# Gathering the expert inputs feature-major for two packs at once in a two-layer decoder step

## The chip, the cores and the metric

The kernel runs on one core of one Trainium2 chip. The metric is the device time of one execution in microseconds (us), as the median of several runs. The five engines are named as in the profile: PE is the matrix engine's products, PEld its weight loads, DVE the vector engine, ACT the scalar engine, POOL the GpSimd engine, and SP the queue that issues nearly all loads.

## The reference

One step of a decoder trunk of two layers over 288 tokens: 256 prompt tokens and 32 decode tokens (8 sequences of 4). Layer 0 mixes with a gated convolution, layer 1 with retention; both have cross-attention into 256 memory tokens, and both end in the mixture of experts that the change is about:

```python
def hier_moe(h, w_group, w_router, w_gate_up, w_down):
        ...
        g = jnp.argmax(lg, axis=-1)
        ...
        topv, topi = lax.top_k(pe, TOP_K_IN_GROUP)
        wts = topv / jnp.sum(topv, axis=-1, keepdims=True) * pg_sel[:, None]
        ...
        gate = jnp.sum(jax.nn.one_hot(eidx, N_EXPERTS, dtype=jnp.float32) * wts[..., None], axis=1)
        gu = jnp.einsum('td,edf->tef', hs, w_gate_up)
        act = jax.nn.silu(gu[..., :EXPERT_FF]) * gu[..., EXPERT_FF:] * gate[..., None].astype(hs.dtype)
        return jnp.einsum('tef,efd->td', act, w_down)
```

Each token picks one of 4 groups and in it 2 of 8 experts (32 experts, model width 1024, expert width 256). Everything is float32.

## The kernel before

**Layout.** The residual `xT` is held feature-major: 8 tiles (KD) of 128 features by 288 tokens. The mixture of experts does not run every expert on every token. It gives each expert 32 slots (CAP) and works through the 32 experts in 8 packs (PACKS) of 4 experts (PK), so that a pack has 128 slots. A pack whose experts have more than 32 tokens would take a further pass (the `spill` code), which these inputs do not need.

**One pack, in the order of PE's program (`experts`).**
1. `gate_up_chunk`, four times: 8 feature tiles by 4 experts, each product a 128x32 piece of `xgT` (the pack's tokens, feature-major) against 512 columns of weights (line 604).
2. `pick(i + 1)`: the tokens of the next pack are gathered by products with a one-hot matrix. Six products: the one-hot of 128 tokens by 128 slots stands as weights, and 512 features of the token rows `htok` move (line 582). There are three token blocks (128, 128 and 32 tokens) and two halves of the features. The result is slot-major (`xg`), so it has to be turned.
3. In packs 1, 3 and 5 of layer 0: `memory_kv`, keys and values for layer 1 (lines 401 and 406), work that fills the stage.
4. `turn_gates`, `turn_act` (lines 620, 625).
5. `combine(i - 1)`: eight products that spread the previous pack's rows back to the tokens (line 636); DVE adds them to `xT` (line 1397).
6. `turn_x(i + 1)`: eight 128x128 transposes of `xg` (line 630); ACT and DVE copy the banks out twice, once between `pick` and `turn_x` (lines 1102, 1410), once behind it (lines 1106, 1414).
7. `down_half`, twice (line 614).

The last pack differs: `combine(i - 1)` stands ahead of its fourth `gate_up_chunk`, and its own `combine` is split around the second `down_half`.

**Ahead of the packs.** `project_out` (line 496) makes the residual of the eight feature tiles. Between its products it calls `turn_scaled` (line 521), which turns one feature tile to token rows by three transposes, and `partial_sums` (lines 530, 534). `last_sums` (lines 543, 548) closes the router's logits and the tokens' mean squares. `route` makes the ranks of the tokens in their experts by three products (lines 562 to 565); around them stand `memory_kv(1, 0)` and `memory_kv(1, 1)` in layer 0 and three filling products in layer 1. DVE turns the ranks into one-hot matrices (`chosen_slots`).

**Loads.** All weights come through a ring of 7 slots of 2 MB, in the order of `SEQ`: per pack four `gu` chunks and two `dn` chunks, with one `kv1` chunk in packs 1, 3 and 5 of layer 0. SP issues the load of a chunk when the chunk 7 places earlier in the ring has been used (`wait_used`, issue at line 357), strictly in order. Five `gu` chunks (`EXTRA`) have places of their own beside the ring (line 344). In layer 0 the first load behind the ring's first seven, `gu` (0, 1, 0), waits for the slot of `kv1` 0, which is free at the end of `memory_kv(1, 1)`; in layer 1 it waits for the last tile of `project_out`.

## Time and profile before

| | us |
|---|---|
| median of 3 runs | 1237.73 (1232.91 to 1238.44) |
| the profiled execution, its own time | 1237.39 |
| its span, first to last instruction | 1235.6 |
| PE busy | 1170.5 (95%) |
| DVE busy | 356.5 (29%) |
| ACT busy | 154.2 (12%) |
| mean granted clock of TensorE | 0.986 |
| moved by DMA | 364.59 MB, mean 295 GB/s |

PE is busy nearly all the time, but a share over the whole span mixes stages. The two mixtures of experts lie at about 321 to 558 us and 1013 to 1226 us. A float32 product appears in the trace as two records, a transpose as one. In the views below, a "chain" is followed back from the last instruction, each step to what released it.

### The profile page before, as it was taken

Reading aid. Unit: us, or ns where it says so; the run is one execution under the profiler, and the core shown is the slowest. Engines: PE = TensorE matmul, PEld = TensorE weight load, DVE = VectorE, ACT = ScalarE, POOL = GpSimd, SP = SyncE. Lnnn points to the kernel's source line nnn. Section 1 sums busy time; section 2 is a strip of 40 time slices with the busy share of each in tenths; the row PEclk is TensorE's granted clock in tenths of the full one; section 3 lists DMA queues with packets and bytes.
Section 4 is the critical chain, followed back from the end, with each engine's and each line's share of the span. In section 5 each row is a group of like instructions: output and inputs, shape, how many; then the busy total and the mean of one; then the engine's idle time right before and its main releaser. Section 6 shows DMA issues by size and latency. Waiting matters only on the chain.

```text
span 1235.6 us, 13751 instructions
## 1 busy us (share of the span) xinstructions
PE 1170.5 (95%) x5928; PEld 689.7 (56%) x5928; DVE 356.5 (29%) x870; ACT 154.2 (12%) x363; POOL 11.8 (1%) x22
## 2 busy tenths in 40 slices
PE   6999999999999998989999999999999999997886
PEld 5567776677554342436655656566667753432333
DVE  4222224112213141335224242424301022432225
ACT  2000002012111110110201011010200021110002
POOL 0000000000000000000000000000000000000000
PEclk9999999999999999999999999999999999999898
DMA  9953336833599999999234657392985469999994
GB/s 384 427 186 136 136 136 282 340 136 136 234 426 424 428 429 427 429 426 427 109 136 191 243 190 294 137 356 115 414 363 186 155 245 428 412 428 427 427 428 169
DMA packets 28159, 364.59 MB, mean 295 GB/s; under 512 B 3280, under 2 KB 3296, under 8 KB 5056
## 3 DMA queue, kind: packets, MB, share of 16 engines
q1 hardware_dynamic: 25200, 339.87, 67.2%
q10 hardware_dynamic: 1712, 19.17, 3.7%
q0 software_dynamic: 1184, 4.63, 1.0%
q8 instruction: 49, 0.80, 0.3%
q14 instruction: 14, 0.11, 0.0%
HBM read 339.34 MB, written 24.32 MB: 294 GB/s over the span
## 4 chain that ended last, share of the span: by engine, by line
PE 85%; DMA 12%; DVE 2%; issue 1%; ACT 1%; SPq 0%; DVEq 0%
PE bank L766 23%; PE bank L496 13%; DMA ring<-in_gu 11%; PE bank L604 7%; PE bank L582 5%; PE bank L401 5%; PE bank L849 5%; PE bank L406 4%; PE bank L636 4%; PE bank L614 3%; PE bank L820 1%; PE bank L452 1%; PE bank L930 1%; PE bank L419 1%; PE bank L475 1%; PE bank L911 1%
## 5 line engine op out<-in xcount | busy, mean ns | idle before, releaser
L766 PE MATMUL bank<-hT,ring 128*128 128x288 f32 x1088 | 268.2, 407 | 0.9 <-issue 0.9
L766 PEld LDWEIGHTS bank<-hT,ring 128*128 128x128 f32 x1088 | 205.7, 190 | 66.9 <-issue 12.0
L496 PE MATMUL bank<-arena,ring 128*128 128x288 f32 x640 | 158.5, 407 | 1.8 <-DVEq L1305 1.8
L496 PEld LDWEIGHTS bank<-arena,ring 128*128 128x128 f32 x640 | 120.2, 190 | 34.2 <-issue 2.2
L604 PE MATMUL bank<-ring,arena 128*32 128x512 f32 x944 | 115.3, 629 | 24.2 <-DMA ring<-in_gu 24.2
L582 PE MATMUL bank<-arena 128*128 128x512 f32 (+1 forms) x192 | 96.5, 628 | 0.2 <-DVE arena L1380 0.2
L604 PEld LDWEIGHTS bank<-ring,arena 128*32 128x32 f32 x944 | 30.4, 113 | 101.2 <-issue 82.5
L636 PE MATMUL bank<-arena 128*128 128x288 f32 x256 | 68.8, 413 | 2.8 <-issue 2.4
L401 PE MATMUL bank<-arena,ring 128*128 128x256 f32 x256 | 60.1, 398 | 9.4 <-DMA ring<-in_wkv 9.4
L582 PEld LDWEIGHTS bank<-arena 128*128 128x128 f32 (+1 forms) x192 | 31.5, 189 | 65.0 <-issue 63.9
L1397 DVE TENSOR_TENSOR xT<-xT,bank 128x288 f32<-128x288 f32 x128 | 58.2, 455 | 33.0 <-PE bank L636 29.2
L401 PEld LDWEIGHTS bank<-arena,ring 128*128 128x128 f32 x256 | 51.1, 201 | 17.7 <-DMA ring<-in_wkv 9.4
L636 PEld LDWEIGHTS bank<-arena 128*128 128x128 f32 x256 | 46.2, 190 | 24.2 <-issue 8.0
L614 PE MATMUL bank<-ring,arena 128*32 128x512 f32 x512 | 58.7, 596 | 1.0 <-DVE arena L1440 1.0
L849 PE MATMUL bank<-ring,hT 128*128 128x512 f32 x128 | 57.2, 597 | 0.0
L406 PE MATMUL bank<-ring,arena 128*128 128x512 f32 x128 | 55.6, 594 | 0.0
L1525 DVE SCALAR_TENSOR_TENSOR ring<-ring,bank 128x512 f32<-128x512 f32 x64 | 39.7, 682 | 46.2 <-PE bank L820 46.2
L1313 DVE TENSOR_TENSOR xT<-xT,bank 128x288 f32<-128x288 f32 x16 | 7.3, 455 | 154.7 <-PE bank L496 154.7
L406 PEld LDWEIGHTS bank<-ring,arena 128*128 128x128 f32 x128 | 24.2, 190 | 30.8 <-issue 30.7
L849 PEld LDWEIGHTS bank<-ring,hT 128*128 128x128 f32 x128 | 23.8, 190 | 30.8 <-issue 30.4
L1391 DVE SCALAR_TENSOR_TENSOR arena<-arena,bank 128x256 f32<-128x256 f32 x16 | 6.7, 419 | 111.1 <-ACT arena L1115 111.1
L614 PEld LDWEIGHTS bank<-ring,arena 128*32 128x32 f32 x512 | 14.8, 109 | 32.2 <-issue 30.6
(245 smaller groups left out, 846.4 us busy)
## 6 DMA issues: line engine op xcount, KB each, us to landing
ring<-in_gu SPq DMA_DIRECT2D x59, 2048.0 KB, 22.0
ring<-in_dn SPq DMA_DIRECT2D x32, 2048.0 KB, 19.8
ring<-in_rin SPq DMA_DIRECT2D x14, 2048.0 KB, 13.2
ring<-in_cin SPq DMA_DIRECT2D x8, 2048.0 KB, 24.5
ring<-in_kc SPq DMA_DIRECT2D x8, 2048.0 KB, 7.7
ring<-in_vc SPq DMA_DIRECT2D x8, 2048.0 KB, 10.5
ring<-in_st SPq DMA_DIRECT2D x8, 2048.0 KB, 10.4
out_rs<-ring ACTq DMA_DIRECT2D x8, 2048.0 KB, 8.4
```

The lines of the kernel that those rows point to most:

```text
L401: mm = pe.matmul(bank[KV_BANKS[i][j]][:, o * NM:(o + 1) * NM], w[:, k, f:f + P], src[:, k, :], start=(k == 0), stop=(k == KD - 1), skip_gr ...
L406: mm = pe.matmul(bank[KV_BANKS[i][j]][:, :], src[:, k, mb * P:(mb + 1) * P], w[:, k, :], start=(k == 0), stop=(k == KD - 1))
L419: mm = pe.matmul(bank[0][32 * h:32 * h + 32, 0:NM], qm[:, 2 * h + dt, 32 * b:32 * b + 32], k2[:, bi, 2 * h + dt, :], start=(b == 0 and dt ...
L496: mm = pe.matmul(bank[1 + o % 4][:, 0:T], w[:, k, :], cat[:, k, :], start=(k == 0), stop=(k == kt - 1))
L582: mm = pe.matmul(bank[n][:, :], sel[0:m, b, :], htok[b][0:m, n * 512:(n + 1) * 512], start=(b == 0), stop=(b == 2))
L604: mm = pe.matmul(bank[2][32 * e:32 * e + 32, :], xt[:, k, 32 * e:32 * e + 32], wv[e // 2][:, e % 2, kk, :], start=(k == 0), stop=(k == KD ...
L614: mm = pe.matmul(bank[5 + n][32 * e:32 * e + 32, :], actT[:, f, 32 * e:32 * e + 32], wv[:, e, f, :], start=(f == 0), stop=(f == 1), skip_g ...
L636: return pe.matmul(bank[b][:, 0:T], yo[:, o * P:(o + 1) * P], GT, start=True, stop=True)
L766: mm = pe.matmul(outs[o], w[:, o, k, :], src[:, k, :], start=(k == 0), stop=(k == KD - 1))
L849: mm = pe.matmul(bank[4 + b][:, :], hT[:, k, b * P:(b + 1) * P], w[:, k, :], start=(k == 0), stop=(k == KD - 1))
L1397: return dve.tensor_tensor(xT[:, o, :], xT[:, o, :], bank[b][:, 0:T], ALU.add)
L1525: dve.scalar_tensor_tensor(out=st[:, j, dt, :], in0=st[:, j, dt, :], scalar=float(np.exp(NS * LOGG[h])), in1=bank[j][:, :], op0=ALU.mult, ...
```

## The change

- `turn_scaled` makes two transposes and one plain product: the 32 decode tokens of feature tile k go to partitions 32 (k // 2) to 32 (k // 2) + 31, so that the decode rows `htok3` fill four partition quarters with 256 features each. `token_sums` writes the decode tokens' sums of squares to all four quarters (six products for three).
- The ranks take five products for three; two of them make the decode ranks and the decode choice for every quarter, with a new constant `tri3` of 128 columns (`iota` and `valid` go). DVE copies the decode choice out and makes the decode ranks in an instruction of its own.
- `picked`, `turn_picked`, `pick` and `turn_x` go, and so does `xg`. Instead the token rows stand as weights and the one-hot of two packs (256 columns) moves: `gather_prompt`, four calls of four products, and `gather_decode`, eight products with 32 rows each, one per partition quarter and column half. The result is feature-major already; ACT and DVE copy each bank out once, two feature tiles by two packs.
- The gather for packs 2j and 2j+1 stands in pack 2j-1; that for packs 0 and 1 is spread over the head and pack 0. In even packs `combine(i - 1)` is split in five and three tiles, around the transposes.
- `combine` takes banks by pack (`SPREAD`); `yo`, `xgT` and the one-hots move to other places in the arena. The order of the loads, the ring and the places beside it stay as they are.

```diff
-    cols = [("ident", P), ("ones", P), ("tri", P), ("iota", NE), ("cos", T), ("sin", T),
-            ("decay", H * 2 * P), ("dmask", TD), ("inner", H * NS), ("tail", 2 * H), ("kvm", 2 * H), ("fold", P),
-            ("neghalf", 3), ("valid", 3), ("thr", PASSES - 1), ("slots", CAP)]
+    cols = [("ident", P), ("ones", P), ("tri", P), ("cos", T), ("sin", T),
+            ("decay", H * 2 * P), ("dmask", TD), ("inner", H * NS), ("tail", 2 * H), ("kvm", 2 * H), ("fold", P), ("tri3", P),
+            ("neghalf", 3), ("thr", PASSES - 1), ("slots", CAP)]
...
-        SPREAD = ((2, 3, 4), (0, 1, 4))
+        X_BANKS = (0, 1, 5, 6)
+        SPREAD = {i: (2, 3, 4) if i % 2 == 0 else (0, 1, 4, 6) for i in range(PACKS)} | {PACKS - 2: (0, 1, 4),
+                                                                                         PACKS - 1: (2, 3, 4)}
...
                 if k >= 2:
                     pe.wait_ge(S("htok_out"), KD * i + k - 1)
-                for b, (t0, n) in enumerate(BLK):
-                    mm = pe.transpose(bank[5 + 2 * (k % 2)][0:n, b * P:(b + 1) * P], hT[:, k, t0:t0 + n], C("ident"))
-                mm.then_inc(S("h_turned"), 1)
+                for b in range(2):
+                    pe.transpose(bank[5 + 2 * (k % 2)][:, b * P:(b + 1) * P], hT[:, k, b * P:(b + 1) * P], C("ident"))
+                g = slice(32 * (k // 2), 32 * (k // 2) + 32)
+                pe.matmul(bank[5 + 2 * (k % 2)][g, 2 * P:3 * P], hT[:, k, TP:T], C("ident"), start=True, stop=True,
+                          skip_group_check=True).then_inc(S("h_turned"), 1)
+
...
+            def token_sums(k):
+
+                for b in range(2):
+                    pe.matmul(bank[1][:, b:b + 1], sq[:, k, b * P:(b + 1) * P], C("ones")[:, 0:1],
+                              start=(k == 0 and b == 0), stop=(k == KD - 1), skip_group_check=True)
+                for g in range(4):
+                    mm = pe.matmul(bank[1][32 * g:32 * g + 32, 2:3], sq[:, k, TP:T], C("ones")[:, 0:1],
+                                   start=False, stop=(k == KD - 1), skip_group_check=True)
+                return mm
...
-                pe.matmul(bank[5][:, 0:3 * NE], C("tri"), M, start=True, stop=False, skip_group_check=True)
-                pe.matmul(v3(bank[5][:, NE:3 * NE], 2), C("ones"), M[:, 0:1, :].to_broadcast([P, 2, NE]), start=False,
+                ranks = v3(bank[5][:, 0:4 * NE], 4)
+                pe.matmul(ranks[:, 0:2, :], C("tri"), M[:, 0:2, :], start=True, stop=False, skip_group_check=True)
+                pe.matmul(ranks[:, 1:3, :], C("ones"), M[:, 0:1, :].to_broadcast([P, 2, NE]), start=False,
                           stop=False, skip_group_check=True)
-                pe.matmul(bank[5][:, 2 * NE:3 * NE], C("ones"), M[:, 1, :], start=False, stop=True,
+                pe.matmul(ranks[:, 2, :], C("ones"), M[:, 1, :], start=False, stop=False, skip_group_check=True)
+                pe.matmul(ranks[:, 2, :], C("tri3", TD), M[0:TD, 2, :], start=False, stop=True, skip_group_check=True)
+                pe.matmul(ranks[:, 3, :], C("fold", TD), M[0:TD, 2, :], start=False, stop=True,
                           skip_group_check=True).then_inc(S("ranks"), 1)
...
-            def picked(sel, n):
-
-                for b, (t0, m) in enumerate(BLK):
-                    mm = pe.matmul(bank[n][:, :], sel[0:m, b, :], htok[b][0:m, n * 512:(n + 1) * 512],
-                                   start=(b == 0), stop=(b == 2))
+            def gather_decode():
+
+                for q in range(2):
+                    for g in range(4):
+                        r = slice(32 * g, 32 * g + 32)
+                        pe.matmul(bank[X_BANKS[g]][:, 256 * q:256 * q + 256], htok3[r, P * q:P * q + P],
+                                  onehot_m[r, 2, :], start=(q == 0), stop=False, skip_group_check=True)
+
+            def gather_prompt(m):
+
+                for b in range(2):
+                    for q in range(2):
+                        k = 2 * m + q
+                        mm = pe.matmul(bank[X_BANKS[m]][:, 256 * q:256 * q + 256], htok[b][:, k * P:(k + 1) * P],
+                                       onehot_m[:, b, :], start=False, stop=(b == 1), skip_group_check=True)
                 return mm
...
-            def turn_picked(n, src):
-                for k in range(4):
-                    mm = pe.transpose(bank[n][:, k * P:(k + 1) * P], src[:, (4 * n + k) * P:(4 * n + k + 1) * P],
-                                      C("ident"))
-                return mm
-
...
-                def pick(i):
-                    pe.wait_ge(S("selected"), PACKS * L + i + 1)
-                    for n in range(2):
-                        picked(onehot_m, n).then_inc(S("x_picked"), 1)
-
-                def turn_x(i):
-                    pe.wait_ge(S("xg_out_a"), PACKS * L + i + 1)
-                    turn_picked(0, xg).then_inc(S("xg_turned"), 1)
-                    pe.wait_ge(S("xg_out_d"), PACKS * L + i + 1)
-                    turn_picked(1, xg).then_inc(S("xg_turned"), 1)
+                def gather(j):
+
+                    pe.wait_ge(S("selected"), PACKS * L + 2 * j + 2)
+                    pe.wait_ge(S("y_out_a"), PACKS * L + 2 * j - 1)
+                    pe.wait_ge(S("y_out_d"), PACKS * L + 2 * j - 1)
+                    gather_decode()
+                    for m in range(4):
+                        gather_prompt(m).then_inc(S("x_done"), 1)
+
+                def gathered(c):
+                    pe.wait_ge(S("xt_out_a"), 9 * L + min(c + 1, 3))
+                    if c == 3:
+                        pe.wait_ge(S("xt_out_d"), 7 * L + 1)
 
                 def combine(i, part=range(KD)):
 
+                    banks = SPREAD[i]
+                    n = len(banks)
                     pe.wait_ge(S("gt_out"), PACKS * L + i + 1)
                     for o in part:
                         if o == 0:
                             pe.wait_ge(S("y_out_a"), PACKS * L + i + 1)
                         if o == 0 and i:
                             pe.wait_ge(S("y_added"), KD * PACKS * L + KD * i)
-                        if o == 4:
+                        if o == (4 if i == PACKS - 1 else 0):
                             pe.wait_ge(S("y_out_d"), PACKS * L + i + 1)
-                        if o == 1 and i != PACKS - 2:
+                        if o == 1 and 3 in banks:
                             pe.wait_ge(S("actT_out"), PACKS * L + min(i + 2, PACKS))
-                        if o >= 3:
-                            pe.wait_ge(S("y_added"), KD * PACKS * L + KD * i + o - 2)
-                        spread(o, SPREAD[i == PACKS - 2][o % 3]).then_inc(S("spread"), 1)
-
-                pe.wait_ge(S("htok_scaled"), 3 * (L + 1))
-                pick(0)
-                turn_x(0)
+                        if o >= n:
+                            pe.wait_ge(S("y_added"), KD * PACKS * L + KD * i + o - n + 1)
+                        spread(o, banks[o % n]).then_inc(S("spread"), 1)
+
-                pe.wait_ge(S("htok_scaled"), 3 * (L + 1))
-                pick(0)
-                turn_x(0)
+                pe.wait_ge(S("selected"), PACKS * L + 1)
+                pe.wait_ge(S("htok_scaled"), 3 * L + 1)
+                gather_decode()
+                pe.wait_ge(S("selected"), PACKS * L + 2)
+                pe.wait_ge(S("htok_scaled"), 3 * L + 3)
+                for m in range(2):
+                    gather_prompt(m).then_inc(S("x_done"), 1)
                 for i in range(PACKS):
                     if i == PACKS - 1:
                         pe.wait_ge(S(f"npass{L}"), 1)
                         more = pe.value_load(npass[0:1, L:L + 1], min_val=0, max_val=PASSES - 1)
-                    pe.wait_ge(S("xt_out_a"), PACKS * L + i + 1)
+                    if i and i % 2 == 0:
+                        pe.wait_ge(S("xt_out_a"), 9 * L + i + 3)
+                        pe.wait_ge(S("xt_out_d"), 7 * L + i + 1)
                     if i >= 2:
                         pe.wait_ge(S("y_added"), KD * PACKS * L + KD * (i - 1))
                     for c in range(4):
-                        if c == 2:
-                            pe.wait_ge(S("xt_out_d"), PACKS * L + i + 1)
+                        if i == 0:
+                            gathered(c)
                         if c == 3 and i == PACKS - 1:
                             combine(i - 1)
-                        gate_up_chunk(c, gate_up_landed(L, i, c), xgT).then_inc(S("gu_sum"), 1)
+                        gate_up_chunk(c, gate_up_landed(L, i, c), xgT[:, :, P * (i % 2):P * (i % 2) + P]) \
+                            .then_inc(S("gu_sum"), 1)
+                        if i == 0 and c < 2:
+                            gather_prompt(2 + c).then_inc(S("x_done"), 1)
                     if i == 0:
                         count_chosen()
-                    if i + 1 < PACKS:
-                        pick(i + 1)
+                    if i == 1:
+                        pe.wait_ge(S(f"npass{L}"), 1)
+                    if i % 2 and i + 1 < PACKS:
+                        gather((i + 1) // 2)
+                    if i and i % 2 == 0:
+                        combine(i - 1, range(5))
                     if L == 0 and i == 0:
                         pe.wait_ge(S("kv1_out"), 2)
                     if L == 0 and i in MEMORY_IN:
@@ -698,11 +742,15 @@
                     turn_gates().then_inc(S("gt_turned"), 1)
                     pe.wait_ge(S("act_ready"), PACKS * L + i + 1)
                     turn_act().then_inc(S("act_turned"), 1)
-                    if i and i < PACKS - 1:
+                    if i % 2 and i < PACKS - 1:
                         combine(i - 1)
-                    if i + 1 < PACKS:
-                        turn_x(i + 1)
+                    if i and i % 2 == 0:
+                        combine(i - 1, range(5, KD))
                     pe.wait_ge(S("actT_out"), PACKS * L + i + 1)
+                    if i and i % 2 == 0:
+                        pe.wait_ge(S("y_added"), KD * PACKS * L + KD * i)
+                    if i % 2 and i + 1 < PACKS:
+                        pe.wait_ge(S("xt_out_a"), 9 * L + i + 4)
...
-                for b, (t0, n) in enumerate(BLK):
-                    act.activation(htok[b][0:n, :], htok[b][0:n, :], ACT.Copy, scale=rstd3[0:n, b:b + 1]) \
-                       .then_inc(S("htok_scaled"), 1)
+                for b, rows in ((2, htok3), (0, htok[0]), (1, htok[1])):
+                    act.activation(rows, rows, ACT.Copy, scale=rstd3[:, b:b + 1]).then_inc(S("htok_scaled"), 1)
...
+                def gathered_out(j, m):
+                    act.wait_ge(S("x_done"), 16 * L + 4 * j + m + 1)
+                    act.activation(xgT[:, 2 * m:2 * m + 2, :], v3(bank[X_BANKS[m]][:, :], 2), ACT.Copy) \
+                       .then_inc(S("xt_out_a"), 1)
+
+                for m in range(3):
+                    gathered_out(0, m)
...
-                def select(i):
-                    chosen_slots(PK * i).then_inc(S("selected"), 1)
+                def select(j):
+                    chosen_slots(2 * PK * j, 2 * PK, slice(2, 3)).then_inc(S("selected"), 1)
+                    chosen_slots(2 * PK * j, 2 * PK, slice(0, 2)).then_inc(S("selected"), 1)
```

## Rows read from the trace of the kernel before

**Rows 1.** The page, part 2: DMA share in tenths and GB/s, in 40 slices of 30.9 us.
```profile
DMA  9953336833599999999234657392985469999994
GB/s 384 427 186 136 136 136 282 340 136 136 234 426 424 428 429 427 429 426 427 109 136 191 243 190 294 137 356 115 414 363 186 155 245 428 412 428 427 427 428 169
```
**Rows 2.** The page, part 4: the chain that ended last, by line.
```profile
PE bank L766 23%; PE bank L496 13%; DMA ring<-in_gu 11%; PE bank L604 7%; PE bank L582 5%; PE bank L401 5%; PE bank L849 5%; PE bank L406 4%; PE bank L636 4%; PE bank L614 3%; PE bank L820 1%; PE bank L452 1%; PE bank L930 1%; PE bank L419 1%; PE bank L475 1%; PE bank L911 1%
```
**Rows 3.** Windows of 10 us: length, then PE, PEld, DVE, ACT, POOL busy (instructions), granted clock, DMA share, GB/s.
```profile
310.00:320.00 10.00, 10.00 (x51) 8.89 (x50) 3.07 (x15) 2.84 (x13) 0.00 (x0) 1.00 0.00 0
...
330.00:340.00 10.00, 10.00 (x66) 3.62 (x59) 1.44 (x6) 0.98 (x2) 0.00 (x0) 1.00 1.03 434
...
530.00:540.00 10.00, 7.79 (x69) 2.62 (x62) 1.00 (x2) 0.35 (x1) 0.00 (x0) 1.00 1.00 425
...
1060.00:1070.00 10.00, 10.00 (x84) 3.02 (x76) 1.54 (x3) 0.96 (x2) 0.00 (x0) 1.00 0.95 374
```
**Rows 4.** Timeline of the SP queue: start us, length, issues of loads, with count.
```profile
302.02 0.33 SPq L357 DMA_DIRECT2D ring<-in_dn  x1
321.11 0.33 SPq L357 DMA_DIRECT2D ring<-in_gu  x1
...
1004.68 0.33 SPq L357 DMA_DIRECT2D ring<-in_gu  x1
...
1041.08 19.23 SPq L357 DMA_DIRECT2D ring<-in_dn  x2
```
**Rows 5.** The chain in order of time, 296 to 345 us: start us, length, line, records.
```profile
296.68 0.48 PE bank L521 x3
...
299.10 0.49 PE bank L530 x6
...
313.89 0.20 PE bank L565 x2
314.09 6.99 PE bank L401 x32
...
342.99 0.87 PE bank L630 x8
```
**Rows 6.** The same chain, packs 2 and 3 of layer 0.
```profile
391.41 5.93 PE bank L582 x12
398.77 3.66 PE bank L636 x14
403.30 3.57 PE bank L614 x32
406.87 6.87 PE bank L604 x64
413.74 5.93 PE bank L582 x12
419.67 13.95 PE bank L406 x32
```
**Rows 7.** The same chain in layer 1: products with 32 rows, four partition quarters at once.
```profile
652.43 1.07 PE bank L820 x8
```
**Rows 8.** Timeline of PE: start us, length, line, records, [idle before <- releaser].
```profile
537.05 1.92 PE L604 MATMUL bank<-ring,arena 128*32 128x512 f32 x16 [2.21 <-DMA ring<-in_gu]
538.91 4.15 PE L636 MATMUL bank<-arena 128*128 128x288 f32 x16
...
1172.59 1.92 PE L604 MATMUL bank<-ring,arena 128*32 128x512 f32 x16 [2.34 <-DMA ring<-in_gu]
1177.39 2.89 PE L604 MATMUL bank<-ring,arena 128*32 128x512 f32 x16 [2.88 <-DMA ring<-in_gu]
...
1201.95 3.55 PE L604 MATMUL bank<-ring,arena 128*32 128x512 f32 x16 [2.08 <-DMA ring<-in_gu]
```
**Rows 9.** Windows of 2 us, columns as in rows 3.
```profile
1202.00:1204.00 2.00, 2.00 (x12) 0.65 (x16) 0.00 (x0) 0.00 (x0) 0.00 (x0) 0.53 0.96 410
...
1206.00:1208.00 2.00, 2.00 (x10) 1.53 (x9) 1.67 (x4) 0.00 (x0) 0.00 (x0) 1.00 0.98 418
```

172 lines of the change are left out of this document (80 added, 92 removed).

## Prediction

> **What bounds the kernel now.** I read the page first. PE is busy 95% of the span and the product lines fill the chain by line, so on the page this looks like a PE kernel from which 6% of gathering (5% in line 582, more in line 630) could be cut. But that line also holds 11% of "DMA ring<-in_gu" [rows 2], and the slices show where it lies: DMA stands at 9 in slices 11 to 18 and 33 to 38, with 412 to 430 GB/s, which is exactly where the two mixtures of experts run [rows 1]. Everywhere else the share is mostly 3 to 6. So I took windows of 10 us. Layer 0: DMA idle at 310 to 320, share 1.00 or more in every window from 330 to 560 (the first and one of the last stand in the rows). PE is also full at 330, but not at 530, where it is busy 7.79 of 10 us. Layer 1 is the same from 1010 to 1210, with one dip to 0.95 and 374 GB/s at 1060 [rows 3]. A share of 1.00 at 427 GB/s is the most that this transfer path shows anywhere in the run.
>
> The timeline of PE says who waits for whom: PE stands before a gate-up product until the `gu` chunk has landed, 2.21 us at 537.05, and in layer 1 2.34, 2.88 and 2.08 us (six more waits of over 1 us, at 470.79, 475.58, 1113.89, 1118.69, 1143.24 and 1148.04, are not shown) [rows 8]. So at the end of both stages the stream of weights is late, not PE.
>
> A balance shows the same. A chunk of 2.10 MB at 427 GB/s takes 4.9 us. A pack is six chunks, 29.5 us; two packs of layer 0 with a `kv1` chunk are 13 chunks, 63.9 us. On PE, a pack repeats after 413.74 - 391.41 = 22.3 us, and one with `memory_kv` takes some 14 us more [rows 6]: 58.7 us for two packs of layer 0 and 44.7 for two of layer 1. PE is the faster of the two already. It looks full in layer 0 because it starts behind: the stage begins with seven loaded slots to eat.
>
> Hence the rule that I use: the end of each stage is the time at which SP may issue the first load of the stream, plus a fixed number of bytes at 427 GB/s, plus what PE does behind the last landings. The first issues are at 321.11 (released by the end of `memory_kv(1, 1)`, which starts at 314.09 and takes 6.99 us [rows 5]) and at 1004.68 (released by the last tile of `project_out`) [rows 4].
>
> **The gather itself: a large saving under cover.** Removed for two packs: 2 x 5.93 us of line 582 [rows 6] and 2 x 0.87 us of line 630 [rows 5], 13.6 us. Added: 16 products with 256 columns, 32 records. The trace has such a record in line 401, 6.99 / 32 = 0.218 us [rows 5], so 7.0 us. The 8 decode products have 32 rows each in four quarters; line 820 has such products with 512 columns, 8 records in 1.07 us [rows 7]. Here 16 records of half the columns, again 1.07 us. If the quarters did not run together it would be 16 x 0.218 = 3.5 us. Sum 8.1 us (bound 10.5): two packs become 5.5 us shorter, 22 us per layer, 44 us in all. One copy out for each bank in place of two shortens ACT and DVE, which wait anyway. All of this lies behind the stream of weights and I cost it at nothing: PE will only wait longer for `gu` chunks. The cover is 63.9 - 53.2 us for two packs in layer 0 and 58.9 - 39.2 us in layer 1; nothing short of those would bring the gather back on the path.
>
> One place gains. In layer 1 the second `dn` load of pack 2 is issued 19 us after the first, at about 1060 [rows 4], when the first half of pack 1's `down_half` frees the slot, and the queue had run dry: the dip at 1060. With the head and pack 0 having one gather of 8.1 us in place of two picks and two turns, and pack 1 8.1 in place of 6.8, PE gets there some 4.5 us sooner, and the dip goes. It is worth 0.5 us by the share (5% of 10) and 1.3 us by the rate (12% of 10) [rows 3]; I take 0.9.
>
> **The order in odd packs.** The eight-microsecond gather now stands ahead of `down_half`, in layer 0 with 14 us of `memory_kv` behind it. Does a slot come free too late? A `dn` chunk lands 9.8 us behind the last `gu` chunk; PE then has 8.1 + 14 + 1 + 3.7 us to do before `down_half` ends 3.6 us later, 18 us behind the landing. The ring allows six chunks, 29.4 us. So nothing runs dry. The wait for the copies of banks 5 and 6 ahead of `down_half` has `turn_act` and `combine` over it, some 5 us against a copy of 0.7. Free.
>
> **What is added ahead of the stream.** This is on the path, since PE is full there and the first load waits for it.
> - `turn_scaled`: three records take 0.48 us [rows 5]. The third, a transpose in one record, becomes a product in two: one more record of 128 columns, 0.11 us from 0.87 / 8 for the transposes of line 630. I take 0.12, bounds 0.08 and 0.2. Seven calls lie before the issue in layer 1 (0.84 us), eight in layer 0 (0.96 us).
> - `token_sums`: six records take 0.49 us [rows 5]; now twelve, of which eight are narrow and in four column quarters. I take +0.3 us a call, bounds 0.1 and 0.8. One call in layer 1, two in layer 0.
> - Ranks: two more products, each 0.20 us like line 565 [rows 5]: +0.4 us (0.2 to 0.6), in layer 0 only, since in layer 1 the first load has been issued by then.
> - The constants grow by 93 columns, 48 KB at 384 GB/s [rows 1]: +0.12 us at the start.
> Together layer 0 +1.96 us (1.0 to 3.8), layer 1 +1.14 us (0.7 to 2.2), start +0.12. DVE's extra copy and its own instruction for the decode ranks stand before the first gather, not before a load: hidden.
>
> The Trainium skill (TensorEngine Tiling, Tiling Modes, Key Properties) says that changing the tiling mode drains the engine, which speaks against four-quarter products between full ones. The trace has the case: 1.07 us for the 8 records of line 820 where their columns alone need 0.85. A drain of 0.2 us at each change would add some 2 us more before each stream; the upper bounds above hold about half of that.
>
> **Behind the last landing.** The code there is the same: gate-up chunk 2 at 537.05 and 1201.95, then `combine(6)`, chunk 3, the turns and the down halves. What may change is PE's clock. At 1201.95 the same 16 records take 3.55 us, against 1.92 at 537.05 [rows 8]; the granted clock is 0.53 there, that is mostly 1.2 GHz, and 1.00 again under `combine(6)`, 2.4 GHz [rows 9]. PE had waited 2.08 us before it, and 2.21 us before the fast one, so equal waits end either way. The change makes PE wait about 3 us before each of pack 7's chunks (4.9 less 1.9), not before one only. In layer 0, where the chunk was fast, I expect the slow one more often than not: +1.3 us, bounds 0 and 3.3 (1.63 for the chunk and as much again for half of `combine`). In layer 1, where it was slow already: 0, bounds -1.6 and +1.7.
>
> **Sum** against the profiled execution's own 1237.39 us: +0.12 +1.96 +1.14 -0.9 +1.3 = +3.6, so 1241.0. The median of the runs is 0.34 above that execution: 1241.3. With all low ends it is 1.1 us less than before, with all high ends 10.6 more.
>
> **The rivals.**
> - *The saving arrives* (faster). If PE set the end of both stages, 44 us would go: about 1194 us. For it: PE is full from 330 to 470 and line 582 is in the chain. Against it: the DMA share in the same windows, and the waits for `gu` behind them. It decides if the stream has slack, and it has only the dip. Chance 0.06.
> - *The clock stays down* (slower). PE in pack 7 works 1.9 of every 4.9 us; if the clock falls in the first wait and doesn't come back until `combine(6)` is over, chunk 2 costs 1.63 us more in layer 0 and `combine(6)` 4.15 us more in both layers: 9.9 in place of 1.3, 1249.9 us. For it: 2.88 us of waiting at 1177.39 already gave 2.89 us for a chunk of 1.92 [rows 8]. Against it: each slow chunk in the trace is followed by work at or near full speed. It decides where PE's busy share in pack 7 falls too low for the grant to return. Chance 0.12.
> The Trainium skill (TensorE: Matmul & The Clock Gate, HAM oscillation) tells of a kernel whose short bursts between transfer waits all ran cold. By that rule every burst of pack 7 would be at 1.2 GHz, as in this rival.
> - *The gather isn't cheaper*: the quarters run one after another, or changes between full and quarter products cost as much as the transposes did. Then two packs take 44.7 or 58.7 us as now, still below the stream: 1241 us as well, and only the lengths in the trace would differ. Chance 0.04.
> - The forecast, stream plus head and tail, has 0.78, with a range of its own from 1236.6 to 1248.4.
>
> **How the numbers follow.** A measurement of this kernel tells about 0.5%, 6.2 us, from no change: below 1231.5 is faster, above 1243.9 slower. Slower: the clock rival's 0.12 and about 0.10 from the forecast's upper half. Faster: 0.07. The range 1235.0 to 1248.0 leaves out the fast rival, most of the clock rival and some of the scatter that the three runs show on the low side.
>
> **What would show each step.** Right: gate-up waits for `gu` of about 3 us each in packs 3 to 7 of both layers; the total of that wait over 60 us; PE's busy time down by some 45 us; DMA at 1.00 from the first issue on without the dip; first issues about 2 us and, in layer 1, a further 1 us later against the stage's start. Wrong: a DMA share below 1.00 inside the stages, a first issue later by more than 4 us, or stages that end earlier against their first issue by more than 2 us.

## The result and the profile after

The changed kernel takes 1249.78 us (median of 4 runs, 1249.41 to 1251.08) against 1236.97 us for the kernel before, run beside it on the same chip: ratio 1.0108, 95% interval 1.0094 to 1.0122. The forecast was 1241.3 us, 1235.0 to 1248.0. It is slower by 12.8 us where I expected 3.6, and outside the range. The profiled execution has a span of 1248.3 us against 1235.6, so the traces show 12.7 of the 12.8 us.

The page of the kernel after: busy time, the GB/s line that answers to [rows 1], the chain by line that answers to [rows 2], and three groups of products of gate-up, the gather and down (busy, mean ns | idle before, releaser).

```profile
PE 1148.7 (92%) x6040; PEld 701.6 (56%) x6040; DVE 341.0 (27%) x854; ACT 146.5 (12%) x347; POOL 11.8 (1%) x22
...
GB/s 383 428 177 135 135 135 319 307 123 135 234 428 427 428 426 427 428 427 399 90 122 196 245 155 333 135 344 114 405 370 162 175 208 428 428 427 427 427 428 163
...
PE bank L812 23%; DMA ring<-in_gu 13%; PE bank L498 13%; PE bank L636 5%; PE bank L403 5%; PE bank L895 4%; PE bank L408 4%; PE bank L604 4%; DMA ring<-in_dn 3%; PE bank L662 3%; PE bank L646 3%; PE bank L866 1%; PE bank L454 1%; PE bank L421 1%; PE bank L976 1%; PE bank L477 1%
...
L636 PE MATMUL bank<-ring,arena 128*32 128x512 f32 x944 | 126.8, 673 | 48.3 <-DMA ring<-in_gu 48.3
...
L604 PE MATMUL bank<-arena 128*128 128x256 f32 x256 | 58.6, 384 | 0.0
...
L646 PE MATMUL bank<-ring,arena 128*32 128x512 f32 x512 | 60.7, 610 | 7.3 <-issue 3.6
```

The share and the rate in both stages are as before (426 to 428 GB/s in most slices), the products of the gather (line 582 before, 604 now) shrink in the chain, and the waits for weights grow in it: gate-up waits 48.3 us for `gu` chunks, and `dn` chunks now bound too. PE is busy 21.8 us less in all. The windows of 10 us answer to [rows 3]: the idle window at 310, the full ones behind it, and at 1060 no dip any more.

```profile
310.00:320.00 10.00, 10.00 (x52) 8.88 (x51) 1.68 (x7) 2.25 (x7) 0.00 (x0) 1.00 0.09 38
...
330.00:340.00 10.00, 10.00 (x76) 4.32 (x68) 0.69 (x1) 0.60 (x1) 0.00 (x0) 1.00 0.99 419
530.00:540.00 10.00, 5.63 (x36) 1.09 (x32) 0.69 (x1) 0.00 (x0) 0.00 (x0) 0.83 1.02 431
...
1060.00:1070.00 10.00, 9.97 (x61) 6.16 (x63) 5.22 (x11) 1.61 (x3) 0.00 (x0) 1.00 1.00 426
```

The gather itself, in the timeline of PE (start us, length, line, records, [idle before <- releaser]). It ends at 424.51, where `memory_kv` begins: 8.1 us from 416.42, as forecast. The three waits above it answer to [rows 6], where PE had none.

```profile
404.80 2.88 PE L636 MATMUL bank<-ring,arena 128*32 128x512 f32 x16 [2.59 <-DMA ring<-in_gu]
409.67 3.27 PE L636 MATMUL bank<-ring,arena 128*32 128x512 f32 x16 [1.99 <-DMA ring<-in_gu]
414.57 1.92 PE L636 MATMUL bank<-ring,arena 128*32 128x512 f32 x16 [1.62 <-DMA ring<-in_gu]
416.42 1.15 PE L596 MATMUL bank<-arena 32*128 32x256 f32 x16
417.50 7.17 PE L604 MATMUL bank<-arena 128*128 128x256 f32 x32
424.51 13.90 PE L408 MATMUL bank<-ring,arena 128*128 128x512 f32 x32
```

**Where 12.7 us came from.** I laid the same marks over both traces: the first issue of each stage [rows 4], the last gate-up chunks [rows 8], and the first product behind the stage.

| stretch | us |
|---|---|
| ahead of layer 0's `project_out` | -0.6 |
| head of layer 0, to the first issue (321.11, now 324.45) | +3.9 |
| stream of layer 0 (537.05, now 540.44, both at full clock) | 0 |
| handover from layer 0 to layer 1 | +6.1 |
| a second wait of PE in layer 1, line 421, at 884 | +0.8 |
| head of layer 1, to the first issue (1004.68, now 1017.91) | +3.0 |
| stream of layer 1, the dip gone | -1.8 |
| tail of layer 1 | +1.2 |

The two first issues, from the timeline of the SP queue:

```profile
324.45 0.33 SPq L359 DMA_DIRECT2D ring<-in_gu  x1
...
1017.91 0.33 SPq L359 DMA_DIRECT2D ring<-in_gu  x1
```

And the handover, from the timelines of PE: the last `combine` of layer 0, then the first product of retention (line 766 before, 812 now). First the kernel before:

```profile
554.86 2.18 PE L636 MATMUL bank<-arena 128*128 128x288 f32 x8 [0.86 <-issue]
558.21 4.12 PE L766 MATMUL bank<-arena,ring 128*128 128x288 f32 x16 [1.17 <-DVE arena L1585]
```

Then the kernel after:

```profile
558.24 2.18 PE L662 MATMUL bank<-arena 128*128 128x288 f32 x8 [0.86 <-issue]
565.86 5.90 PE L812 MATMUL bank<-arena,ring 128*128 128x288 f32 x16 [5.44 <-issue]
```

PE is idle 5.44 us in place of 1.17, no event in the trace releases it ("issue"), and the 16 records behind it take 5.90 us in place of 4.12. This stretch alone is half of the loss, and the prediction has no term for it.

The second wait is small and lies far from any changed product, between line 419 (now 421) and the line behind it. The kernel before, then the kernel after:

```profile
867.05 7.11 PE L419 MATMUL bank<-ring,arena 128*32 128x256 f32 x128 [1.03 <-DVE arena L1256]
874.09 1.99 PE L431 MATMUL bank<-arena 128*128 128x256 f32 x8
...
876.48 7.11 PE L421 MATMUL bank<-ring,arena 128*32 128x256 f32 x127 [1.03 <-DVE arena L1295]
884.01 0.40 PE L421 MATMUL bank<-ring,arena 128*32 128x256 f32 x1 [0.43 <-issue]
884.34 1.99 PE L433 MATMUL bank<-arena 128*128 128x256 f32 x8
```

From start to start that is 7.86 us in place of 7.04. The last record again waits for nothing that the trace shows.

### The profile page after: what moved, and what is told of

It reads as the page before. It is cut to its first block, busy times and chain, and to the rows that moved or that the text cites. A ratio compares the mean times of both kernels' runs of the same rounds, so it can differ in the third digit from the quotient of the medians.

```text
span 1248.3 us, 13951 instructions
## 1 busy us (share of the span) xinstructions
PE 1148.7 (92%) x6040; PEld 701.6 (56%) x6040; DVE 341.0 (27%) x854; ACT 146.5 (12%) x347; POOL 11.8 (1%) x22
## 4 chain that ended last, share of the span: by engine, by line
PE 80%; DMA 16%; DVE 2%; issue 1%; ACT 1%; SPq 0%; DVEq 0%
PE bank L812 23%; DMA ring<-in_gu 13%; PE bank L498 13%; PE bank L636 5%; PE bank L403 5%; PE bank L895 4%; PE bank L408 4%; PE bank L604 4%; DMA ring<-in_dn 3%; PE bank L662 3%; PE bank L646 3%; PE bank L866 1%; PE bank L454 1%; PE bank L421 1%; PE bank L976 1%; PE bank L477 1%
## 5 line engine op out<-in xcount | busy, mean ns | idle before, releaser
L636 PE MATMUL bank<-ring,arena 128*32 128x512 f32 x944 | 126.8, 673 | 48.3 <-DMA ring<-in_gu 48.3
L646 PE MATMUL bank<-ring,arena 128*32 128x512 f32 x512 | 60.7, 610 | 7.3 <-issue 3.6
L662 PEld LDWEIGHTS bank<-arena 128*128 128x128 f32 x256 | 46.2, 190 | 26.2 <-issue 13.0
L604 PE MATMUL bank<-arena 128*128 128x256 f32 x256 | 58.6, 384 | 0.0
L604 PEld LDWEIGHTS bank<-arena 128*128 128x128 f32 x256 | 47.8, 190 | 12.3 <-issue 6.3
```

Source lines behind the costliest of these rows:

```text
L604: mm = pe.matmul(bank[X_BANKS[m]][:, 256 * q:256 * q + 256], htok[b][:, k * P:(k + 1) * P], onehot_m[:, b, :], start=False, stop=(b == 1), ...
L636: mm = pe.matmul(bank[2][32 * e:32 * e + 32, :], xt[:, k, 32 * e:32 * e + 32], wv[e // 2][:, e % 2, kk, :], start=(k == 0), stop=(k == KD ...
L646: mm = pe.matmul(bank[5 + n][32 * e:32 * e + 32, :], actT[:, f, 32 * e:32 * e + 32], wv[:, e, f, :], start=(f == 0), stop=(f == 1), skip_g ...
L662: return pe.matmul(bank[b][:, 0:T], yo[:, o * P:(o + 1) * P], GT, start=True, stop=True)
```

## The experiments

Theory A for the heads: the narrow product of `turn_scaled` costs several times what I gave it. Theory B for the handover: what PE waits for is its own instructions behind the branch that skips the further pass. The rivals were that the head is longer for the sums and the ranks, and that the gather's own work, its waits or the clock made the difference. Ratios are to the kernel before on the same chip.

### The heads: the decode tokens turned by a product or by a transpose

In the kernel after, the plain product goes and a transpose that ends on the same partitions takes its place. Everything else stays.

```diff
-                pe.matmul(bank[5 + 2 * (k % 2)][g, 2 * P:3 * P], hT[:, k, TP:T], C("ident"), start=True, stop=True,
-                          skip_group_check=True).then_inc(S("h_turned"), 1)
+                n = 32 * (k // 2) + 32
+                pe.transpose(bank[5 + 2 * (k % 2)][0:n, 2 * P:3 * P], hT[:, k, T - n:T], C("ident")) \
+                  .then_inc(S("h_turned"), 1)
```

> The changed kernel with its decode turn made by a transpose of the last 32, 64, 96 or 128 tokens of the feature tile, so that the 32 decode tokens still land in their partition quarter but no product on a 32-column part of the array is needed. Theory A (the head): each of the 16 decode turns by a narrow product costs 0.42 us of PE on the path to the first load of a stage (a period of 9.27 us for 8.85), so the first load of layer 0 comes about 3 us earlier than in the changed kernel (324.45 to about 321.4) and of layer 1 another 3 us; the time falls by 6 us to about 1244. Rival: the head is longer for the sums and the ranks; then the first loads move by less than 1 us each and the time stays within 2 us of 1249.8.

Measured: 1241.55 us, ratio 1.0042 (1.0023 to 1.0060), 8.2 us less. The first issues are at 321.92 and 1012.58. The counterpart gives the kernel before the plain product for its third transpose:

```diff
-                for b, (t0, n) in enumerate(BLK):
-                    mm = pe.transpose(bank[5 + 2 * (k % 2)][0:n, b * P:(b + 1) * P], hT[:, k, t0:t0 + n], C("ident"))
-                mm.then_inc(S("h_turned"), 1)
+                for b in range(2):
+                    pe.transpose(bank[5 + 2 * (k % 2)][:, b * P:(b + 1) * P], hT[:, k, b * P:(b + 1) * P], C("ident"))
+                pe.matmul(bank[5 + 2 * (k % 2)][0:TD, 2 * P:3 * P], hT[:, k, TP:T], C("ident"), start=True, stop=True,
+                          skip_group_check=True).then_inc(S("h_turned"), 1)
```

> The kernel before with one thing taken from the change: the turn of the 32 decode tokens of each feature tile is a plain product instead of a transpose; everything else stays. Theory A: the period of a feature tile in project_out grows from 8.85 to about 9.27 us, both stages' first loads come 3 us later each, and the time rises by 5 to 7 us to about 1243. Rival (one more record of 128 columns, 0.11 us): the period grows by 0.12 us and the time by 1.5 to 2 us.

Measured: 1243.03 us, 1.0053 (1.0033 to 1.0074), 6.5 us more, first issues at 323.74 and 1010.57. Sixteen times 0.42 us are 6.7 us, and that is what the kernel before loses. The kernel after gains 1.5 us more; in its trace with the transpose the second wait, at line 421, is gone as well, which is 0.8 us of it. The timeline shows how the 0.42 us come about. After:

```profile
289.28 0.44 PE L523 MATMUL bank<-cst,hT 128*128 128x128 f32 x2
289.65 0.41 PE L525 MATMUL bank<-cst,hT 128*32 128x128 f32 x2
289.99 8.03 PE L498 MATMUL bank<-arena,ring 128*128 128x288 f32 x32
297.94 0.68 PE L515 MATMUL bank<-hT,arena 128*36 128x288 f32 x2
```

With the transpose:

```profile
287.85 0.44 PE L523 MATMUL bank<-cst,hT 128*128 128x128 f32 x2
288.13 0.27 PE L525 MATMUL bank<-cst,hT 128*96 128x128 f32 x1
288.24 7.93 PE L498 MATMUL bank<-arena,ring 128*128 128x288 f32 x32
296.09 0.68 PE L515 MATMUL bank<-hT,arena 128*36 128x288 f32 x2
```

From start to start, the transpose takes 0.11 us, the narrow product 0.34, the two transposes ahead of it 0.37 in place of 0.28, and the 32 records of line 498 take 7.95 in place of 7.85. So the narrow product costs 0.42 us more, and the surplus lies on both of its sides as well as in it. The number of columns alone does not bring it: the transposes for the first two feature tiles have 32 columns too (128*32), and the first of them, in layer 0, also takes 0.11 us (243.90 to 244.01). A plain product of 128 columns in the same place was not tried.

### The handover: the branch, then where its target lies

First the branch of PE alone is taken away, with the further pass that it skips (these inputs never use it).

```diff
-                with pe.If(more > 0):
+                if False:
```

> The changed kernel without the branch in PE's program around the further pass, which is not taken with these inputs; the code of that pass on PE is left out. Theory B (handover): the 5.4 us in which PE stands idle at 560.4 to 565.9, behind the last pack of layer 0 and with the rin chunk landed at 560.0, is a fetch of instructions behind the branch, that has to queue in the full DMA rings. Without the branch that wait is gone or below 1.5 us, the following 16 products run at the full clock (4.1 for 5.9 us), and the time falls by 5 to 6.5 us to about 1244. Rival: PE waits there for data or for another engine; then the idle time stays at 4 us or more and the time within 1.5 us of 1249.8.

> The kernel before without the branch in PE's program around the further pass; that pass's code on PE is left out. Theory B: PE waits only 1.17 us there, for DVE's first scaled tile, so nothing is to be gained: the same within 1 us. If the branch costs something by itself in both kernels, the time falls here too by 2 us or more, and the difference between the two kernels isn't explained by it.

Measured: the kernel after 1243.79 us, 1.0060 (1.0043 to 1.0077), idle 1.18 us and released by DVE, 4.12 us for the product; the kernel before 1236.58 us, 1.0003. So the wait comes with the branch, and only the kernel after pays it. In the kernel after without the branch:

```profile
561.38 4.12 PE L812 MATMUL bank<-arena,ring 128*128 128x288 f32 x16 [1.18 <-DVE arena L1625]
```

Both kernels have the branch. What differs is the code around it. A first pair was to move the code with 128 empty instructions at the start of PE's program (`pe.nop()`).

> The changed kernel with 128 empty instructions at the start of PE's program, where PE waits for its first weights until 9.4 us anyway. Theory B (a fetch of instructions whose cost depends on where the branch's target lies in the fetched blocks): the idle time of 5.4 us at the handover from layer 0 to layer 1 changes, to below 2 us in the likelier case, and the time falls by 4 to 6 us. Rival (a wait for data or an engine): nothing moves, within 1.5 us of 1249.8, since no other work is changed.

> The kernel before with the same 128 empty instructions at the start of PE's program. Theory B: where the target now lies unluckily, an idle time of 4 us or more appears behind the last pack of layer 0 and the time rises by 4 to 6 us; otherwise the same within 1 us. Rival: the same within 1 us in any case.

Measured: 1251.30 and 1235.95 us, idle times as without them. The profile lists as many instructions as for the unshifted kernels (13951 in the one after), and its instruction queue holds as many packets (51 and 49). So nothing shows that the empty instructions moved anything, and the pair tells nothing. A second pair changed how far the branch jumps: in the kernel after the skipped code loses 18 products (six calls of `gather_single`, three products each), in the kernel before it gains fifteen.

```diff
-                            for k in range(KD):
+                            for k in range(2):
                                 mm = gather_single(k)
```

> The changed kernel with the code of the further pass on PE (jumped over, never run with these inputs) shortened by 18 of its 24 gather products, to 67 products, which is fewer than the 75 of the kernel before; the changed kernel has 85. Theory B2: what matters is how far the branch jumps; a near target is fetched already, a far one has to be fetched through the full DMA rings. Then the idle time of 5.4 us behind layer 0 falls to 1.2 us and the time by 5 to 6.5 us, as without the branch. Rival B3 (the branch as such, or its place in the program): the wait stays above 4 us and the time within 1.5 us of 1249.8.

```diff
-                            picked(onehot_m, 0)
+                            for _ in range(6):
+                                picked(onehot_m, 0)
```

> The kernel before with the jumped-over code of the further pass on PE lengthened by 15 products, from 75 to 90, none of which is run. Theory B2: an idle time of 4 us or more appears on PE behind the last pack of layer 0, and the time rises by 5 to 6 us to about 1242. Rival B3: the same within 1 us.

Measured: 1250.88 us with 5.34 us idle, and 1236.54 us with 1.17. The length of the jump alone is not it.

```profile
q8 instruction: 1, 0.02, 6.3%
```

The kernel after, first 535 to 563 us (no q8 line), then 563 to 564, where `combine` had ended at 560.4:

```profile
q1 hardware_dynamic: 824, 11.98, 100.6%
q14 instruction: 1, 0.01, 0.1%
...
q1 hardware_dynamic: 28, 0.43, 99.9%
q8 instruction: 1, 0.02, 6.6%
```

The branch itself stands in the traces at 556.12 us before and at 559.51 after. So before, a fetch comes 5.6 us ahead of the branch; after, none comes in the 24.8 us ahead of it, the next 3.6 us behind it, and PE works 2 us later. A real shift was made with products of one column at PE's start, where it waits until 9.4 us for its first weights:

```diff
+            pe.wait_ge(S("par_in"), 16)
+            for _ in range(24):
+                pe.matmul(bank[7][0:32, 0:1], par[:, 0:32], par[:, 0:1], start=True, stop=True)
             memory_kv(0, 0)
```

> The kernel after with 24 one-column products more at the start of PE's program, where PE waits for the first weights until 9.4 us anyway; they cost nothing there and move everything behind them by 96 instructions. Theory F (what PE waits for at the handover is the fetch of its own instructions behind the branch: the branch of pack 7 comes near the end of a fetched piece of 16 KB, 256 instructions, and its target lies in a piece that is asked for only when PE jumps): the branch now lies behind a piece border, the piece with the target is asked for before the jump, the fetch record at 564.9 us moves to before 558, the idle time ahead of the first product of retention goes from 5.4 us to about 1.2 us, released by DVE, that product takes 4.1 us in place of 5.9, and the time is 1243.5 to 1246 us. Theory G (the wait belongs to the branch itself, or to work that only the kernel after has, wherever the code lies): 5.4 us again, and 1249.5 to 1251.5 us.

> The kernel after with 64 one-column products more at the same free place: 256 instructions, exactly one piece, so that all code lies in its piece where it lay before. Theory F: the wait stays, 5.4 us, and the time is 1249.5 to 1251.5 us. If any insertion at the start removes the wait (theory H, some other effect of the inserted products), the idle time is about 1.2 us here as well, 1243.5 to 1246 us.

> The kernel before with 46 one-column products more at the same free place, 184 instructions. In the kernel before the piece with the branch's target is asked for at 552.2 us, five us ahead of the branch. Theory F: the border moves to behind the branch, the fetch comes only after the jump, and an idle time of 4 to 5.5 us appears ahead of the first product of retention where 1.17 us stood; 1240.5 to 1243 us. Theory G: 1.17 us again, and 1235.5 to 1238 us.

Measured: 24 products in the kernel after, 1243.13 us, 1.0060 (1.0042 to 1.0078); 64 products, a whole piece, 1250.70 us, 1.0133 (1.0107 to 1.0159); 46 products in the kernel before, 1236.74 us, 1.0011. The first two are as theory F says: 96 instructions at a place where PE has nothing to do make the kernel 6.6 us faster than the kernel after (7.6 us faster than its neighbour with 256 on the same chip), 256 do nothing. With 96 the wait at line 421 is gone too, and from the first product of retention to the first issue of layer 1 the kernel takes 3.0 us more than the kernel before, not 3.8; with 256 that wait is there again, 0.43 us. So the second wait hangs on the place of the code as well. The third run missed: no wait came. Counting the products then put some 296 instructions between branch and target in the kernel before and 351 in the kernel after, and gave a sharper rule, which the next two runs were made to break.

> The kernel before with 30 one-column products at the free place at the start, 120 instructions. A count of PE's instructions puts some 296 between the branch and its target in the kernel before and some 351 in the kernel after. The fetch times of the shifted kernels fit one rule (F2): PE holds the piece in which it works and has the next one asked for when it enters it; a jump is free if its target lies in one of these two, and else it waits for a fetch. In the kernel after the branch's piece ends about 58 instructions behind the branch, so the two reach to 314, short of 351; in the kernel before it ends about 146 behind, so they reach to 402, beyond 296; 184 instructions of shift left 218 and 474, still beyond, which is why that run missed. 120 instructions leave 26 and 282, short of 296. F2: an idle time of 4 to 5.5 us ahead of the first product of retention, with a fetch after the jump, and 1240.5 to 1243.5 us. If the kernel before can't be made to wait by a shift (F only an accident of the kernel after): 1.17 us and 1235.5 to 1238 us.

> The kernel after with 58 one-column products, 232 instructions: less than a piece. F2: the branch's piece ends 82 behind the branch, the two reach to 338, short of 351 by a little: the wait stays, 5.4 us, 1249.5 to 1251.5 us. If what counts is only that the branch isn't in the last part of its piece (58 is near the end, 82 less so), it may be gone: 1.2 us, 1243.5 to 1246 us. The count has some twenty instructions of uncertainty, so this one is the nearer call of the two.

Measured: the kernel before with 30 products 1244.50 us, 1.0059 (1.0038 to 1.0080), the kernel after with 58 products 1248.37 us, 1.0078 (1.0059 to 1.0097) with 5.45 us idle. Both waited, as the rule says; the times lie 1.0 us above and 1.1 us below what was expected. The first product of retention, in the timeline of PE. The kernel after with 24 products (with 64 the idle time is 5.30 us):

```profile
561.83 4.12 PE L812 MATMUL bank<-arena,ring 128*128 128x288 f32 x16 [1.18 <-DVE arena L1628]
```

The kernel before with 30 products (with 46 it is 1.17 us):

```profile
564.55 1.78 PE L766 MATMUL bank<-arena,ring 128*128 128x288 f32 x3 [5.72 <-issue]
```

In its DMA view, the window of 561 to 562 us has the fetch, and 535 to 561 has none; `combine` had ended at 558.8 (556.65 + 2.18):

```profile
q8 instruction: 1, 0.02, 6.7%
```

### Is the gather under cover?

In layer 1 the kernel after keeps 4 of 24 products of each gather in packs 1, 3 and 5; the kernel before leaves out two thirds of the one-hot products for packs 1 to 7. Both leave part of the gather undone.

```diff
-                    gather_decode()
+                    if L == 0:
+                        gather_decode()
                     for m in range(4):
-                        gather_prompt(m).then_inc(S("x_done"), 1)
+                        if L == 0:
+                            mm = gather_prompt(m)
+                        else:
+                            mm = pe.matmul(bank[X_BANKS[m]][:, 256:512], htok[1][:, 0:P], onehot_m[:, 1, :], start=True,
+                                           stop=True, skip_group_check=True)
+                        mm.then_inc(S("x_done"), 1)
...
-                for b, (t0, m) in enumerate(BLK):
+                for b, (t0, m) in enumerate(BLK[0:blocks]):
...
-                        picked(onehot_m, n).then_inc(S("x_picked"), 1)
+                        picked(onehot_m, n, 1 if L and i else 3).then_inc(S("x_picked"), 1)
```

> The changed kernel with most of the gather left out in layer 1: of the 24 products of each gather for packs 2 to 7 only four remain. This takes about 6.9 us of PE three times, 20 us in all. The law of the stream (first load plus bytes plus what follows the last landing): the time stays within 1.5 us of 1249.8, and PE only waits 20 us longer for gate-up weights. If PE's work were on the path, the time would fall by up to 20 us.

> The kernel before with two thirds of the one-hot products left out in layer 1, for packs 1 to 7: 4 us of PE a pack, 28 us in all. The law of the stream: at most the dry spot of the load queue at 1060 us goes, so 0 to 2 us faster than before (1235 to 1237), although 28 us of PE work are gone. If PE's work were on the path: up to 28 us faster.

Measured: 1248.49 and 1234.70 us, 1.3 and 1.8 us less than the kernels that they come from. Some 19 us (three gathers, 8.1 us each, less 1.75 us for the four products that stay) and 28 us (two thirds of seven times 5.93) of PE's work bought next to nothing: in layer 1 the saving of the change is hidden as the forecast said, and the stream sets the stage. In layer 0 nothing was left out; there only the traces speak, with a stream of the same length in both kernels.

### Moving the stream forward

If a stage is its first issue plus bytes, bytes moved ahead of it should count in full. Three `gu` chunks beside the ring were put earlier in the order.

```diff
+for moved, ahead_of in ((("gu", (0, 1, 1)), ("gu", (0, 1, 0))), (("gu", (0, 1, 2)), ("gu", (0, 1, 0))),
+                        (("gu", (1, 1, 1)), ("gu", (1, 0, 0)))):
+    SEQ.remove(moved)
+    SEQ.insert(SEQ.index(ahead_of), moved)
```

> The kernel before with three loads moved in SP's order: the two gu chunks of layer 0 that have a place beside the ring go ahead of the chunk that waits for the slot of kv1 0, and one such chunk of layer 1 goes ahead of layer 1's first gu. The law of the stream: 9.8 us of bytes in layer 0 and 4.9 us in layer 1 move into time in which the queue was idle or half used. But PE of the kernel before has only about 6 us of waits in layer 0 to give up, so I expect 5 to 6 us there and 4 to 5 us in layer 1: 1226 to 1229. If the stream doesn't set the end, within 2 us of before.

> The changed kernel with the same three loads moved. Here PE has some 19 us of waits in layer 0 and more in layer 1, so the stream's whole 9.8 + 4.9 us should be gained: 1249.8 - 14.7 = 1235, 13 to 15.5 us faster than the changed kernel. This is where the cheaper gather would first be worth something: its gain from this edit should be 4 us larger than that of the kernel before.

Measured: 1233.27 us, 0.9975 (0.9962 to 0.9988), and 1246.22 us, 1.0086 (1.0057 to 1.0114): 3.5 and 3.6 us less, where 8 to 15.5 were expected; and the kernel after gains no more than the kernel before, where 4 us more were expected of it. Windows of 5 us show the queue running dry elsewhere. The kernel before with the new order, columns as in [rows 3]:

```profile
325.00:330.00 5.00, 4.80 (x47) 1.70 (x49) 1.55 (x3) 0.60 (x1) 0.00 (x0) 1.00 0.34 102
370.00:375.00 5.00, 4.28 (x20) 2.93 (x19) 0.88 (x2) 0.60 (x1) 0.00 (x0) 1.00 0.43 102
1055.00:1060.00 5.00, 5.00 (x52) 1.47 (x48) 1.97 (x4) 0.60 (x1) 0.00 (x0) 1.00 0.55 164
```

Its SP queue explains the second window:

```profile
372.13 0.33 SPq L361 DMA_DIRECT2D ring<-in_dn  x1
```

and its PE timeline the queue, by `memory_kv` of pack 1:

```profile
358.02 14.08 PE L405 MATMUL bank<-arena,ring 128*128 128x256 f32 x64
```

The `dn` load at 372.13 is issued as `memory_kv` ends (358.02 + 14.08 = 372.10). In the first packs the ring waits for PE, so bytes moved forward are partly lost again; that this is the whole difference between 8 or more and 3.5 us was not separated.

### Together

The transpose, the new order and 28 one-column products (24, and 4 for the 16 instructions that the transposes save) in the kernel after:

> The kernel after with all that the runs so far point to: the decode tokens turned by a transpose (8 us), the three loads beside the ring ahead of their packs (3.6 us), and 28 one-column products at the start (24 as in the first run of this group, 4 for the 16 instructions that the transposes save). Theory F: 1250.2 - 8.2 - 3.6 - 5.5 = about 1233 us, 1231 to 1236, level with the kernel before or a little faster. Theory G: the handover keeps its 5.4 us, and 1237 to 1240 us.

Measured: 1232.38 us, 0.9974 (0.9959 to 0.9988). It beats the kernel before, by 3 us, and is level with the kernel before in the new order (0.9975). The feature-major gather, freed of its side costs, is worth nothing measurable here.

## Why the prediction was wrong

**What bounds the kernel: right.** The stages run at the transfer rate from the first issue on (427 GB/s is what they sustain, not the most that shows: [rows 3] has a window at 434), layer 0's stream has the same length within 0.1 us, and taking gather work away in layer 1 changes under 2 us.

**The gather: right.** 8.1 us for two packs against 8.1 forecast, 13.6 before. The quarters do run together (1.08 us from 416.42 to 417.50). The wait for `gu` doubled, from 24.2 to 48.3 us, but did not pass 60: some of the saving went into slower products, some into waits for `dn`. PE's busy time fell by 21.8 and not by 45 us: gate-up was busy for 126.8 us with the same 944 records (115.3 before), down for 60.7 (58.7), and the longer heads and the slow first product of retention add some 9 us, an estimate from the stretches above.

**The dip: right in kind.** It is gone; layer 1's stream is 1.8 us shorter against its first issue, where I took 0.9 of a range to 1.3.

**The heads: right in kind, wrong in size.** The term `turn_scaled` is the step that failed: 0.12 us a call (bounds 0.08 and 0.2) against 0.42, which is +3.4 us in place of 0.96 for eight calls, and 2.9 in place of 0.84 for seven. I had priced a narrow product as one more record of a transpose, the nearest row by columns but not by tile. `token_sums`, at +0.3 us, was too dear: from start to start it is 0.60 against 0.58. The ranks cost 1.23 against 0.58 us, +0.65 for my 0.4. Head of layer 0: +3.9 for 1.96 forecast, just beyond the upper bound of 3.8; layer 1: +3.0 for 1.14, beyond its 2.2. The prediction had quoted the Trainium skill (TensorEngine Tiling, Tiling Modes, Key Properties), that a change of tiling mode drains the engine, and had set a drain aside at some 2 us per stage, half in the bounds. A drain would fit the 0.42 us, which lie on both sides of the product, but the runs do not show one: the transpose of the same 32 columns cost nothing extra, and a weight load that shows was not ruled out.

**The handover: no step at all.** This is the larger of the two failed steps. The sum ended each stage and began the next as if nothing lay between, a term put at nothing without a reason. It cost 6.1 us: 4.3 of waiting and 1.8 of a product at a lower clock behind it (granted clock 0.63 from 565 to 571 us). The second wait adds 0.8. Nothing in the profile of before points to it; its only trace there is a q8 packet at 550 us. What I could have done is to ask of each branch whether the change moves code around it.

**The clock: neither the term nor the rival came.** The chunk ahead of layer 0's last `combine` ran at full clock, so the +1.3 did not come; PE's waits in that pack were 0.49, 2.89 and 1.43 us before the first three chunks, not 3 us before each, and the four chunks took 1.92, 3.50, 1.92 and 1.92 us, so not every burst ran at 1.2 GHz. In the tail of layer 1 the clock moved elsewhere. Two lines of the timeline of PE answer to [rows 8]: the chunk before `combine(6)`, slow before, is fast now, and a `down_half` that waited for its `dn` chunk takes 3.59 us in place of 1.92.

```profile
1213.41 1.92 PE L636 MATMUL bank<-ring,arena 128*32 128x512 f32 x16 [1.69 <-DMA ring<-in_gu]
...
1224.83 3.59 PE L646 MATMUL bank<-ring,arena 128*32 128x512 f32 x16 [1.21 <-DMA ring<-in_dn]
```

The window of 5 us around the second has a granted clock of 0.68:

```profile
1225.00:1230.00 5.00, 4.24 (x20) 1.17 (x16) 0.06 (x1) 1.50 (x2) 0.00 (x0) 0.68 0.22 93
```

The two cancel (-1.6 and +1.7 us); the net of +1.2 us is what PE now waits for the last `gu` and `dn` chunks. `combine(6)` took 4.15 us in both layers, so the rival in which the clock stays down is refuted, though its 1249.9 us is what was measured: a right number from a wrong mechanism.

**The sum.** The measured terms, -0.6 + 3.9 + 6.1 + 0.8 + 3.0 - 1.8 + 1.2, make 12.6 us. The heads took 3.8 us more than forecast (6.9 for 3.1), the handover and the second wait 6.9; the start and the dip gave 1.6 back. Where the 0.6 us at the start come from was not looked into.

## What to carry over

Where a stream of transfers sets a stage, price every product ahead of its first issue, and price a product of a new kind (a plain product of few columns among full ones) from a row of that kind, or take several times the row at hand as its bound. Work taken off a covered engine is worth nothing until the stream moves, and the stream can move only as far as the early packs free its slots. If a change lengthens or shortens an engine's program ahead of a branch, look in the instruction queue whether the fetch of the target still comes before the jump.

## What the runs showed of the hardware

- **A jump can cost 4.1 to 4.6 us of waiting.** Nine kernels with the branch waited 5.3 to 5.8 us and nine did not (1.17 or 1.18). The traces tell them apart by the instruction queue: in the nine that waited, its last packet ahead of the branch came 21 to 27 us before it, in the nine others 2 to 11 us before it; in all eighteen the next packet came 3.6 to 4.2 us behind the branch.
- **A rule that would explain this fits all runs but one by my counts, and is not shown.** PE would have the 256-instruction piece in which it works and the next one, and would wait for a target in a third. The branch stood at 58 (after) and 26 (before + 30) instructions from the end of its piece with 351 and 296 to jump, where it waited, and at 218 (after + 24) and 146 or 218 (before, before + 46) where it did not. The kernel after with the shorter skipped code speaks against these counts: 18 products less leave 279 instructions to jump, inside 58 + 256 = 314, and it waited 5.34 us. It would fit if the branch stood less than 23 from the end, but the counts rest on products alone and were taken to be off by some twenty at most. Why the fetch takes that long was not tried; the DMA share stands at 1.00 or more in these windows, which may be why.
- **Padding can be free speed.** 96 instructions with no use made one kernel 6.6 us faster, 256 left it as it was, and 120 made the other 7.2 us slower.
- **A plain 128x32 product between full products took 0.42 us more than the transpose that writes the same rows,** with a transpose of 32, 64, 96 or 128 columns at 0.11 us.
- **PE's clock behind a wait is not one number.** After 5.4 us of idling 16 records took 5.90 us in place of 4.12; a chunk of 1.92 us took 1.92 us after 1.69 us of waiting and 3.59 us after 1.21.
